# Layer 0, attention heads 8 to 15: VectorE's low halves of the turned probabilities before the biased maxima two heads on

## The chip, the cores and the metric

The kernel runs on one core of one Trainium2 chip. The metric is device time in microseconds (us) of one execution. The kernel before took 1215.46 us, the median of three runs (1212.08 to 1216.16).

## The reference, cut to what matters

A two-layer decoder trunk on 512 tokens of width 1024, in float32. Layer 0 mixes eight heads of full causal attention with a forget gate (kind A, heads 0 to 7) and eight heads of attention over a sliding window of 128 tokens with a sink and a bias by distance (kind B, heads 8 to 15). The change lies in the stretch of kind B:

```python
logits = jnp.einsum("bnqhgd,bnkhd->bnhgqk", qb, kb) * (d ** -0.5)
logits = jnp.where(mask, logits + bias, -jnp.inf)
sink = jnp.broadcast_to(sinks..., logits.shape[:-1] + (1,))
p = jax.nn.softmax(jnp.concatenate([logits, sink], axis=-1), axis=-1)[..., :-1]
out = jnp.einsum("bnhgqk,bnkhd->bnqhgd", p, vb)
```

The outputs of all sixteen heads go through one output projection, then a squared-ReLU MLP; layer 1 is another mixer and another MLP, and a norm ends it.

## The kernel before, in words

Nothing of the order is planned by a program: each engine has its instructions written out by hand in one in-order stream, and semaphores (`wait_ge`, `then_inc`) tie the streams together. Float32 precision comes from halves: a value is split into a rounded high half (ScalarE, a copy to fp32r, line 1191) and the low half that is left (a subtraction, on VectorE at line 1806 or on GpSimd at line 1628), and TensorE multiplies the halves one after the other. GpSimd also makes the low halves of the weights (wl, 128x1024 each).

Layer 0's attention is run in steps s = -2 to 15; every engine has its own `first_step(s)`. For s from 8 to 15 the step holds, on each engine in this order:

- TensorE (L1012): the scores of head s+2 (L830, L831; they wait for the exponentials of head s+1), the projection slabs of the step (only the last one, slab 18, in step 8) or some tiles of the output projection (`OUT_TILES_AT`, L711 to L713: nine matmuls in each of the steps 9 to 14, six in step 15), the values of head s (L901 with the high halves of the turned probabilities, L902 with the low halves; each bank waits for `pt_lo`), and the transposes of the probabilities of head s+1 (L891; they wait for `probs_ready`).
- ScalarE (L1421): half of the output of head s-1 from its bank (sq, `o_half`), the high halves of head s (probT_h, `pt_hi`), the high half of an earlier output, the exponentials of head s+2 (L1372, four instructions in two banks, and a small one for the sink at L1370, `exp_done`), and in steps 8, 10 and 12 the high half of one weight slab (128x1024).
- VectorE (L2054): the two halves of the output of head s-1 summed (L2045, `o_sum`), `maxima(s + 2)` (L1991: four custom instructions at L2006 that add the bias strip to the scores in their bank and take the row extremum, `max_ready`), `probs_lo(s)` (L2031: two subtractions at L1806, `pt_lo`), `normalise(s + 2)` (L2024: `sums` at L2021 and L2022, which wait for the exponentials of head s+2, then four multiplications at L2029, `probs_ready`), and in steps 7 to 9 the low half of a projected query and its slab (L1806, L1863).
- GpSimd: in steps 8, 10 and 12 the low half of a weight slab, then in even steps the low half of an output pair (128x512, ur<-sq,ur).
- SyncE: weight loads and the bias strips (L641); the strip of head j waits for the maxima of head j-2.

The maxima of head s+2 exist in this place for s = 8 to 13 only (the condition `NH <= s and s + 2 < 2 * NH`, with NH = 8). In steps below 8 the maxima stand in a later place of the step, and steps 14 and 15 have none. Behind step 15 come the last tiles of the output projection, whose later weights are loaded once the last transposes are done (L682, L683, L609).

Of the kernel before, what the change touches and what calls it, by code (L numbers as in the profile page):

```python
# [43 lines left out]
NH = 8  # L44
# [102 lines left out]
def trunk(nc, x, norm_mix_e, w_in_e, b_forget, sink_logits, w_out_e, norm_mix_o, w_in_o, norm_cq, norm_ckv,  # L147
          w_uq, w_ukv, w_out_o, norm_mlp, w_mlp1, w_mlp2, rel_bias, norm_final,
          c_onehot, c_fixed, c_rope, out):
    with ExitStack() as ctx:  # L150
# [279 lines left out]
        def units(j):  # L430
            if attention(j) == "B":
                return [(0, 0, 0, 128, 0), (1, 0, 128, 256, 128), (2, 1, 0, 256, 384), (3, 1, 256, 256, 640)]
            return [(0, 0, 0, 128, 0), (2, 0, 128, 384, 128), (1, 1, 0, 256, 512), (3, 2, 0, 512, 768)]
# [4 lines left out]
        def attention(j):  # L438
            return "ABDC"[j // NH]
# [4 lines left out]
        def banks_before(j):  # L444

            return sum(score_banks(i) for i in range(j))
# [48 lines left out]
        def placed(n):  # L495

            return n + 1 if n < FA else n
# [11 lines left out]
        def slabs_of(s):  # L509
            return SLABS_AT.get(s, ())  # L510
# [18 lines left out]
        def strip_count(j):  # L529

            return sum(1 for i in range(j + 1) if attention(i) in "BC" and i % 2 == j % 2)
# [1266 lines left out]
        def _(dve):  # L1798
# [51 lines left out]
            def take_slab(n, scale=1.0, dst=None):  # L1850
                dve.wait_ge(slab_done, n + 1)
                if n in (N_IN1 + 2, N_IN1 + 3, N_IN1 + 4) and dst is None:
                    dve.wait_ge(p_hi, SPLIT0 + n - N_IN1 - 1)
                    if n == N_IN1 + 2:
                        dve.wait_ge(ki_lo, 1)
                        dve.wait_ge(ki_spread, 1)
                    else:
                        dve.wait_ge(qi_lo, n - N_IN1 - 2)
                elif n >= N_IN1 + 2 and dst is None:
                    dve.wait_ge(p_lo, SPLIT0 + n - N_IN1 - 4)  # L1860
                elif 2 <= n < N_OUT0 and n - 2 != FA and dst is None:
                    dve.wait_ge(p_lo, placed(n - 2))
                v.scalar_tensor_tensor(tbuf[:, n % 2, :] if dst is None else dst, pj(n)[:, :], scale, rstd[:, :], ALU.mult, ALU.mult)\  # L1863
                    .then_inc(slab_taken, 1)
# [126 lines left out]
            def maxima(j):  # L1991
                if j >= 2:
                    dve.wait_ge(exp_done, banks_before(j - 1))
                us, slot = units(j), j % 2
                biased = attention(j) in "BC"
                if biased:
                    dve.wait_ge(strip_loaded[slot], 16 * strip_count(j))
                if j == NH:
                    dve.wait_ge(sink_ready, 1)
                for i, (blk, b, col, w, _) in enumerate(us):  # L2000
                    dve.wait_ge(scores_ready, banks_before(j) + b + 1)
                    logits, neg = bank[b][:, col:col + w], negmax[:, slot, blk:blk + 1]
                    if biased:
                        width = 2 * W if attention(j) == "B" else S
                        limit = sink_neg[:, j % NH:j % NH + 1] if attention(j) == "B" else -TAKEN
                        m = v.tensor_tensor_reduce(logits, logits, strip_raw[:, slot, width - w:width], -1.0, limit,  # L2006
                                                   ALU.add, ALU.min, neg)
                    else:
                        m = v.reduce_max(neg, logits, AX.X, negate=True)  # L2009
                    if i + 1 == len(us) or us[i + 1][1] != b:  # L2010
                        m.then_inc(max_ready, 1)

            def sums(j):

                dve.wait_ge(exp_done, banks_before(j + 1))
                if j >= 2 * NH + 2:
                    dve.wait_ge(diag_made, j - 2 * NH - 1)
                elif j >= 2:
                    dve.wait_ge(probs_ready, 4 * (j - 1))
                if attention(j) == "B":  # L2020
                    own.link(v.tensor_tensor(sink_exp[:, j % 2, :], sink_exp[:, j % 2, :], expsum[:, j % 2, :], ALU.add))  # L2021
                v.reciprocal(rsum[:, j % 2, :], (sink_exp if attention(j) == "B" else expsum)[:, j % 2, :]).then_inc(rsum_ready, 1)  # L2022

            def normalise(j):  # L2024
                sums(j)
                dve.wait_ge(rsum_ready, j + 1)
                for blk, _, _, w, pc in units(j):
                    pr = probs[:, j % 2, pc:pc + w]
                    v.tensor_scalar(pr, pr, rsum[:, j % 2, blk:blk + 1], None, ALU.mult).then_inc(probs_ready, 1)  # L2029

            def probs_lo(s, parts=range(3)):  # L2031

                for k, (b, c0, w) in enumerate(pt_banks(s)):
                    if k not in parts:
                        continue
                    dve.wait_ge(pt_hi, pt_before(s) + k + 1)
                    c = slice(512 * k, 512 * k + w)
                    sub(probT_l[:, c], bank[b][:, c0:c0 + w], probT_h[:, c]).then_inc(pt_lo, 1)

            def outputs_summed(s):  # L2040

                _, r = out_tile(s)
                dve.wait_ge(o_half, s + 1)
                o = o_f32(s)[r:r + HD, :]
                v.tensor_tensor(o, out_bank(s)[HD:P, :], o, ALU.add).then_inc(o_sum, 1)  # L2045
# [8 lines left out]
            def first_step(s):  # L2054

                if 1 <= s:
                    outputs_summed(s - 1)
                if NH <= s and s + 2 < 2 * NH:
                    maxima(s + 2)
                if 0 <= s:  # L2060
                    probs_lo(s, range(2))
                if NH <= s and s + 2 < 2 * NH:
                    normalise(s + 2)
                if s < NH:
                    if 0 <= s:
                        probs_lo(s, (2,))
                    maxima(s + 2)
                    if 0 <= s + 1:
                        normalise(s + 1)
                for n in slabs_of(s - 1):  # L2070
                    if n not in V_INSIDE:
                        projected(placed(n) - 1, EVEN[n][0], n)
                for n in slabs_of(s):
                    take_slab(n, HD ** -0.5 if EVEN[n][0][0] == "q" else 1.0)
                    if n in V_INSIDE:
                        projected(placed(n) - 1, EVEN[n][0], n)
                if s == NH - 1:
                    normalise(NH + 1)
# [91 lines left out]
            for s in FIRST_STEPS:  # L2170
                first_step(s)
# [105 lines left out]
```

## Time and profile before

| what | before |
|---|---|
| median of three runs | 1215.46 us (1212.08 to 1216.16) |
| the profiled execution | 1216.44 us, span 1214.6 us |
| TensorE (matmul) busy | 1166.6 us, 96% |
| VectorE busy | 678.1 us, 56% |
| ScalarE busy | 505.5 us, 42% |
| GpSimd busy | 523.1 us, 43% |
| steps 8 to 15 of the attention | about 161 to 213 us after the span's start |

The span runs from the first to the last instruction of the profiled execution, whose own time is 1.8 us more. In rows of instructions the first column is the start in us from the span's start, the second the time the group lasted; "xN" is the number of instructions merged in a row, and the bracket at the end is the idle time of the engine ahead of it and who ended it. In output<-input the names are the program's. The custom maxima show as CUSTOM_DVE_ANT_0.

### The profile page before, as it was taken

What the parts mean: (1) busy time and instruction counts of PE and PEld (TensorE: products, weight loads), DVE (VectorE), ACT (ScalarE), POOL (GpSimd) and SP (SyncE); (2) the same over time, 40 slices, a digit from 0 to 9 for tenths busy, and PEclk for the clock granted to TensorE, in tenths of its full rate; (3) what the DMA queues carried; (4) which work ended last, traced back from release to release, by engine and by line L of the source; (5) the groups of instructions that cost most, each with busy time, mean ns of one, the idle gap of its engine ahead of it and who ended that gap; (6) DMA issues with size and microseconds to landing.
All of it is one profiled execution on the core that took longest, in us unless ns stands there. A gap on an engine that the chain in (4) does not pass through costs nothing.

```text
span 1214.6 us, 15797 instructions
## 1 busy us (share of the span) xinstructions
PE 1166.6 (96%) x5601; PEld 959.5 (79%) x5605; DVE 678.1 (56%) x1094; ACT 505.5 (42%) x910; POOL 523.1 (43%) x267
## 2 busy tenths in 40 slices
PE   7999988999999999999997899989999999999997
PEld 5788877878888888888765778878788888888886
DVE  5866697664154163265569798737651541631654
ACT  6677665432222132134373377844321321322233
POOL 2433322444444444447643375224444444444441
PEclk9999998999999999999998999999999999999999
DMA  5233331333333333333322100103333333333332
GB/s 158 72 108 94 98 114 46 110 88 100 103 88 105 89 101 99 91 104 87 88 69 70 35 19 27 45 18 87 87 104 90 102 100 91 104 88 102 92 98 87
DMA packets 191225, 104.94 MB, mean 86 GB/s; under 512 B 9062, under 2 KB 187537, under 8 KB 191170
## 3 DMA queue, kind: packets, MB, share of 16 engines
q1 hardware_dynamic: 189900, 104.09, 29.8%
q8 instruction: 33, 0.54, 0.2%
q10 hardware_dynamic: 1270, 0.13, 0.1%
q14 instruction: 22, 0.18, 0.0%
HBM read 102.04 MB, written 6.35 MB: 89 GB/s over the span
## 4 chain that ended last, share of the span: by engine, by line
PE 81%; DVE 9%; ACT 5%; issue 3%; POOL 1%; DMA 1%; SPq 0%; DVEq 0%; ACTq 0%
PE bank L711 25%; PE bank L713 25%; PE bank L712 25%; ACT probs L1372 2%; PE bank L889 2%; DVE probT_l L1806 1%; POOL wl L1628 1%; PE bank L891 1%; PE bank L901 1%; ACT ur L1191 1%; PE bank L902 1%; DVE score L2127 1%; ACT wh L1191 1%; DVE best L2123 1%; DVE probs L2029 1%
## 5 line engine op out<-in xcount | busy, mean ns | idle before, releaser
L1628 POOL TENSOR_TENSOR wl<-raw,wh 128x1024 fp32r<-128x1024 f32 x171 | 417.8, 2444 | 550.0 <-ACT wh L1191 550.0
L711 PE MATMUL bank<-ur,wh 128*128 128x512 f32 x1072 | 418.5, 390 | 0.3 <-POOL wl L1628 0.3
L713 PE MATMUL bank<-ur,wl 128*128 128x512 f32 x1072 | 417.1, 389 | 0.0
L712 PE MATMUL bank<-ur,wh 128*128 128x512 f32 x1072 | 417.1, 389 | 0.0
L1191 ACT ACTIVATE wh<-raw 128x1024 fp32r<-128x1024 f32 x171 | 180.8, 1058 | 509.4 <-PE bank L713 509.2
L711 PEld LDWEIGHTS bank<-ur,wh 128*128 128x128 f32 x1072 | 201.4, 188 | 43.1 <-issue 1.6
L712 PEld LDWEIGHTS bank<-ur,wh 128*128 128x128 f32 x1072 | 201.3, 188 | 42.1 <-issue 0.5
L713 PEld LDWEIGHTS bank<-ur,wl 128*128 128x128 f32 x1072 | 201.2, 188 | 41.6
L1970 DVE TENSOR_TENSOR xT<-bank,xT 128x512 f32<-128x512 f32 x64 | 44.3, 692 | 227.7 <-PE bank L713 227.5
L1806 DVE TENSOR_TENSOR ur<-sq,ur 128x512 fp32r<-128x512 f32 x65 | 129.8, 1997 | 45.4 <-ACT ur L1191 45.4
L711 PE MATMUL bank<-xh,wh 128*128 128x512 f32 (+1 forms) x296 | 123.5, 417 | 7.8 <-POOL xl L1628 3.0
L712 PE MATMUL bank<-xl,wh 128*128 128x512 f32 (+1 forms) x296 | 117.9, 398 | 0.0
L713 PE MATMUL bank<-xh,wl 128*128 128x512 f32 (+1 forms) x296 | 117.5, 397 | 0.0
L1961 DVE TENSOR_TENSOR tbuf<-bank,rstd 128x512 f32<-128x512 f32 x64 | 44.2, 691 | 92.1 <-PE bank L713 91.6
L711 PEld LDWEIGHTS bank<-xh,wh 128*128 128x128 f32 (+1 forms) x296 | 56.6, 191 | 24.6 <-issue 8.5
L1372 ACT ACTIVATE probs<-bank,negmax 128x256 f32<-128x256 f32 (+3 forms) x128 | 63.4, 506 | 27.4 <-DVE negmax L2009 15.2
L1191 ACT ACTIVATE ur<-sq 128x512 fp32r<-128x512 f32 (+1 forms) x80 | 50.6, 633 | 45.9 <-DVE sq L1965 38.5
L713 PEld LDWEIGHTS bank<-xh,wl 128*128 128x128 f32 (+1 forms) x296 | 56.7, 192 | 13.3
L712 PEld LDWEIGHTS bank<-xl,wh 128*128 128x128 f32 (+1 forms) x296 | 57.0, 192 | 12.7 <-issue 1.5
L1870 DVE TENSOR_TENSOR sqsum<-sqsum,sq 128x512 f32<-128x512 f32 x28 | 46.0, 1642 | 18.8 <-ACT sq L1230 18.8
L1806 DVE TENSOR_TENSOR probT_l<-bank,probT_h 128x512 fp32r<-128x512 f32 (+1 forms) x88 | 48.8, 599 | 12.6 <-ACT probT_h L1191 12.4
L1191 ACT ACTIVATE ur<-tbuf 64x512 fp32r<-64x512 f32 (+2 forms) x68 | 42.3, 628 | 26.4 <-DVE tbuf L2108 14.6
(223 smaller groups left out, 1291.6 us busy)
## 6 DMA issues: line engine op xcount, KB each, us to landing
raw<-in_w_mlp SPq DMA_DIRECT2D x128, 512.0 KB, 3.9
raw<-in_w_in_e SPq DMA_DIRECT2D x18, 512.0 KB, 3.7
raw<-in_w_in_o SPq DMA_DIRECT2D x10, 512.0 KB, 3.7
raw<-in_w_out_e SPq DMA_DIRECT2D x8, 512.0 KB, 4.0
raw<-in_w_out_o SPq DMA_DIRECT2D x8, 512.0 KB, 3.7
skew_c<-bias_rows SPq DMA_DIRECT2D x8, 319.5 KB, 4.6
strip_raw<-skew_c SPq DMA_DIRECT2D x8, 256.0 KB, 2.6
skew_b<-bias_rows SPq DMA_DIRECT2D x8, 191.5 KB, 4.0
```

Of the source, the lines that this page charges most:

```text
L711: mm(dst, lhs[0], rhs[0], start=start, stop=False, skip_group_check=not check)
L712: mm(dst, lhs[0], rhs[1], start=False, stop=False, skip_group_check=not check)
L713: return mm(dst, lhs[1], rhs[0], start=False, stop=stop, skip_group_check=not check)
L889: done = mm(dst, probs[:, slot, c:c + P], diag[slot][:, q:q + P], start=True, stop=True)
L891: done = nc.tensor.transpose(dst, probs[:, slot, c:c + P], ident[:, :])
L1191: return nc.scalar.activation(dst, src, ACT.Copy, scale=scale)
L1372: e = nc.scalar.activation(probs[:, slot, pc:pc + w], bank[b][:, col:col + w], ACT.Exp, bias=negmax[:, slot, blk:blk + 1], scale=sign, acc ...
L1628: return nc.gpsimd.tensor_tensor(dst, a, b, ALU.subtract)
L1806: return v.tensor_tensor(dst, a, f(b), ALU.subtract)
L1870: v.tensor_tensor(sqsum[:, :], sqsum[:, :], sq[:, m % 2, :], ALU.add).then_inc(sq_added, 1)
L1961: v.tensor_tensor(t, ps, rstd[:, :], ALU.mult).then_inc(slab_taken, 1)
L1970: v.tensor_tensor(xT[:, m, :], ps, xT[:, m, :], ALU.add).then_inc(slab_taken, 1)
```

## The change

In `first_step` of VectorE the call of `maxima(s + 2)` is moved from ahead of `probs_lo(s, range(2))` to behind it, directly ahead of `normalise(s + 2)`. The condition is the same. No instruction, wait or transfer is added or dropped, and no other engine's stream changes.

```diff
@@ -2055,11 +2055,10 @@
 
                 if 1 <= s:
                     outputs_summed(s - 1)
-                if NH <= s and s + 2 < 2 * NH:
-                    maxima(s + 2)
                 if 0 <= s:
                     probs_lo(s, range(2))
                 if NH <= s and s + 2 < 2 * NH:
+                    maxima(s + 2)
                     normalise(s + 2)
```

## Rows read from the trace of the kernel before

**Rows 1.** The page, busy time of each engine over the span.
```profile
PE 1166.6 (96%) x5601; PEld 959.5 (79%) x5605; DVE 678.1 (56%) x1094; ACT 505.5 (42%) x910; POOL 523.1 (43%) x267
```
**Rows 2.** Waits, 145 to 215 us: us in total, times, longest.
```profile
PE bank L901 <- DVE probT_l L1806: 8.8, 4, 3.8
...
DVE sink_exp L2021 <- ACT probs L1372: 2.1, 6, 0.5
```
**Rows 3.** The chain that ended last, step 11: start, us, what.
```profile
184.94 0.69 DVE sq L2045
...
187.30 0.56 DVE probT_l L1806
187.99 0.37 PE bank L901
```
**Rows 4.** Timeline of VectorE, step 9.
```profile
170.70 0.69 DVE L2045 TENSOR_TENSOR sq<-bank,sq 64x512 f32<-64x512 f32 x1
171.43 0.36 DVE L2006 CUSTOM_DVE_ANT_0 bank<-bank,strip_raw,sink_neg 128x128 f32<-128x128 f32 x1
...
172.92 1.15 DVE L1806 TENSOR_TENSOR probT_l<-bank,probT_h 128x512 fp32r<-128x512 f32 x2
174.55 0.16 DVE L2021 TENSOR_TENSOR sink_exp<-sink_exp,expsum 128x4 f32<-128x4 f32 x1 [0.48 <-ACT probs L1372]
...
174.97 1.07 DVE L2029 TENSOR_SCALAR probs<-probs,rsum 128x128 f32<-128x128 f32 x4
176.07 1.39 DVE L1806 TENSOR_TENSOR ur<-tbuf,ur 64x512 fp32r<-64x512 f32 x2
```
**Rows 5.** Timeline of VectorE, its idle times in steps 12 and 14.
```profile
190.40 0.69 DVE L2045 TENSOR_TENSOR sq<-bank,sq 64x512 f32<-64x512 f32 x1 [0.29 <-ACT sq L1191]
192.12 0.36 DVE L2006 CUSTOM_DVE_ANT_0 bank<-bank,strip_raw,sink_neg 128x128 f32<-128x128 f32 x1 [1.02 <-PE bank L831]
...
204.49 0.69 DVE L2045 TENSOR_TENSOR sq<-bank,sq 64x512 f32<-64x512 f32 x1 [0.47 <-ACT sq L1191]
205.37 1.15 DVE L1806 TENSOR_TENSOR probT_l<-bank,probT_h 128x512 fp32r<-128x512 f32 x2 [0.19 <-ACT probT_h L1191]
```
**Rows 6.** Timeline of TensorE, first value matmul of steps 9, 11, 13 and 14.
```profile
173.75 0.36 PE L901 MATMUL bank<-probT_h,ur 128*128 128x256 f32 x1 [3.85 <-DVE probT_l L1806]
...
187.99 0.37 PE L901 MATMUL bank<-probT_h,ur 128*128 128x256 f32 x1 [2.15 <-DVE probT_l L1806]
...
201.89 0.55 PE L901 MATMUL bank<-probT_h,ur 128*128 128x256 f32 x1 [2.43 <-DVE probT_l L1806]
...
207.28 0.28 PE L901 MATMUL bank<-probT_h,ur 128*128 128x256 f32 x1
```
**Rows 7.** Busy time by stretch; the number behind POOL is the granted clock.
```profile
178.00:179.00 1.00, 1.00 (x7) 0.83 (x6) 0.95 (x4) 0.63 (x1) 0.00 (x0) 1.00 0.01 5
189.00:191.00 2.00, 2.00 (x12) 2.00 (x11) 1.68 (x6) 0.93 (x2) 0.00 (x0) 0.50 0.86 249
```
**Rows 8.** Timeline of ScalarE, high halves of weights, steps 8 and 10.
```profile
165.32 1.06 ACT L1191 ACTIVATE wh<-raw 128x1024 fp32r<-128x1024 f32 x1 [0.41 <-PE bank L713]
...
181.13 1.07 ACT L1191 ACTIVATE ur<-raw 128x1024 fp32r<-128x1024 f32 x1
```
**Rows 9.** Timeline of GpSimd, steps 8 and 10.
```profile
166.46 2.94 POOL L1628 TENSOR_TENSOR wl<-raw,wh 128x1024 fp32r<-128x1024 f32 x1 [6.03 <-ACT wh L1191]
169.36 1.71 POOL L1628 TENSOR_TENSOR ur<-sq,ur 128x512 fp32r<-128x512 f32 x1
182.28 2.48 POOL L1628 TENSOR_TENSOR ur<-raw,ur 128x1024 fp32r<-128x1024 f32 x1 [11.21 <-ACT ur L1191]
```
**Rows 10.** Timeline of VectorE beside those GpSimd instructions.
```profile
166.46 3.49 DVE L1806 TENSOR_TENSOR ur<-tbuf,ur 64x512 fp32r<-64x512 f32 x2
...
181.69 3.22 DVE L2029 TENSOR_SCALAR probs<-probs,rsum 128x128 f32<-128x128 f32 x4
```
**Rows 11.** Timeline of SyncE's queue behind the last transposes.
```profile
209.15 0.38 SPq L682 DMA_DIRECT2D probs<-in_w_uq  x1
...
210.14 12.27 SPq L609 DMA_DIRECT2D raw<-in_w_out_e  x3
```
**Rows 12.** Timeline of TensorE, output projection, the first marked idle behind step 15.
```profile
231.40 0.47 PE L711 MATMUL bank<-ur,wh 128*128 128x512 f32 x1 [0.26 <-POOL wl L1628]
```

## The prediction

> **What bounds the kernel now.** First the page: TensorE is busy for 96% of the span [rows 1], so time can be gained only in the few places where it stands still, and lost wherever it is made to stand still. Then the waits of the stretch from 145 to 215 us, which holds the changed steps: there TensorE's value matmuls wait four times, 8.8 us in all, for VectorE's low halves [rows 2]. That is what the moved call seems to serve. But the wait names only the last releaser. The chain shows what lies behind it: in step 11 it runs along VectorE from the output sum at 184.94 through the maxima to the low half at 187.30, and only then to TensorE at 187.99 [rows 3]. So I read VectorE's own stream over a whole step, to see whether the low halves are late because of the maxima alone, or because VectorE is late as a whole.
>
> Step 9 is the plain one [rows 4]. The output sum starts at 170.70, the maxima 0.73 us later at 171.43, the low halves at 172.92 for 1.15 us; then VectorE idles 0.48 us for ScalarE's exponentials, makes the sums at 174.55, and normalises from 174.97 for 1.07 us. From the start of the maxima to the start of the sums is 174.55 - 171.43 = 3.12 us. This is a chain through two engines: maxima, exponentials, sums. The low halves lie inside it, in time in which VectorE would otherwise wait. All that is spare in the step is 0.48 us. Over the six steps 8 to 13 the waits before the sums come to 2.1 us [rows 2], so in the five others it is (2.1 - 0.48) / 5 = 0.32 us. In this stretch VectorE with that chain is the bound, and TensorE waits for it.
>
> **The change, part by part.** Nothing is added or removed; six calls of the maxima (steps 8 to 13) go behind two low halves each. No DMA is moved on its queue. SyncE's strip for the head two further on waits for these maxima and comes later with them, but has more than 6 us before it is used (the output sums of steps 12 and 14, two steps apart, lie 14.1 us apart [rows 5]).
>
> What is won: in each of the six steps the low halves start earlier by the length of the maxima, 172.92 - 171.43 = 1.49 us [rows 4] to 1.6 us, as the high halves of the head are ready by then in most steps.
>
> What is lost: the maxima start later by the two low halves, 1.15 us and 0.04 us of turnaround, 1.19 us in all. Their exponentials start and end later by the same amount, and so do the sums and the normalising, since nothing on VectorE is left to fill the wait: its idle time there goes from some 0.35 us to some 1.5 us. As the next step's sum of outputs stands behind the normalising in the same stream, the whole next step is later too. So the loss adds up from step to step, and the gain does not. Six steps: 6 x 1.19 = 7.1 us at the end of step 13.
>
> What takes up part of it [rows 5]: in step 12 VectorE idles 0.29 us for ScalarE's half of the output and 1.02 us for the scores; work that is late by more than that finds no wait there, so 1.31 us come back. In step 14 it idles 0.47 us and 0.19 us: 0.66 us. Then TensorE: in step 14 it starts its value matmuls at 207.28 without a wait [rows 6], whereas the low half began at 205.37. In step 9 TensorE started 173.75 - 172.92 = 0.83 us behind the start of the low half, so here it could have started at 206.20, and has 1.08 us of room. Together 3.05 us. Loss at the value matmuls of step 14: 7.14 - 3.05 = 4.1 us. In steps 14 and 15 no maxima are left and nothing changes.
>
> Check against the steps between: the values of step 9 come a little earlier or about level (late by what step 8 loses, 1.2 us, early by 1.5 us [rows 4]); those of step 11 are late by 3 x 1.19 - 1.6 = 2.0 us, those of step 13 by 5 x 1.19 - 1.31 - 1.6 = 3.0 us. TensorE's waits of 3.85, 2.15 and 2.43 us [rows 6] therefore stay in sum.
>
> **GpSimd in step 8** is the part that I can only bound. VectorE instructions between on-chip tiles are held up while GpSimd works: the four normalising instructions of step 10 take 3.22 us beside a weight's low half of 2.48 us [rows 9, 10], as against 1.07 us in step 9 [rows 4], and two projected low halves take 3.49 us as against 1.39 us [rows 4, 10]. In steps 10 and 12 both sides are released by the same exponentials, so the collision moves as it stands: no cost. In step 8 ScalarE's weight half starts at 165.32, released by TensorE [rows 8]; with the exponentials 1.19 us later it starts right behind them, as it does in step 10 at 181.13. Then the last normalising instruction of step 8 meets GpSimd as in step 10 (2.15 us more), the projected low halves meet it no longer (2.10 us less), unless GpSimd's next instruction, the output's low half of 1.71 us [rows 9], meets them in turn. Between nothing and 1.4 us; both engines are engaged the whole time, and I take the middle, 0.7 us.
>
> The Trainium skill ("SBUF — State Buffer", the section on the shared port pair) says that a VectorE instruction in a two-port mode, or with two inputs in SBUF, and a GpSimd instruction exclude each other for a whole instruction, whichever starts first. By that rule both collisions in step 8 would happen in full, and the sum would be 4.1 + 1.4 = 5.5 us; that is the upper end of the bound above.
>
> **Downstream.** The shift passes on in full. Behind step 15 TensorE has no marked idle until 0.26 us at 231.40 [rows 12], and the loads of the later output weights are issued behind the last transposes, from 209.15 [rows 11], so they move along.
>
> **Sum:** 4.1 + 0.7 = 4.8 us over the profiled execution, 1216.44 to 1221.2 us. That execution lies 1.0 us over the median of the runs shown, so against 1215.46 us I forecast 1220.3 us, slower by 0.4%. About 0.3%, 3.6 us here, is what a measurement of this kernel can tell from no change: the forecast lies only just outside.
>
> **Rivals.** *TensorE's side decides (faster).* If VectorE had room, TensorE's waits would shrink by the 1.6 us that the low halves come earlier, in steps 9, 11 and 13, and by the fourth wait of the list, 8.8 - 3.85 - 2.15 - 2.43 = 0.4 us in step 10: 3 x 1.6 + 0.4 = 5.2 us, giving 1210.3 us. A second gain goes with it: behind waits of over 2 us TensorE runs at a granted clock of 0.50, that is 1.2 GHz (189 to 191 us), and at 1.00, 2.4 GHz, elsewhere [rows 7]; shorter waits could spare that. For it speaks the wait list [rows 2]. Against it speaks that VectorE idles only 0.32 to 0.48 us in the place where 1.19 us would be needed. It decides from the point at which the idle ahead of the sums exceeds 1.19 us. Chance 0.08, with a further 0.02 for smaller gains.
>
> *Absorbed.* More of the loss is taken up than I count: ScalarE could work off its copies of outputs and high halves before the delayed exponentials, and a step whose values start earlier has its scores earlier, as in step 12, where the maxima wait for them. If half of the 7.1 us is recovered rather than 3.05 us and step 8 costs nothing, 3.5 us remain; if two steps are free, 1.7 us. 1217 to 1219 us. That also holds if the order as it runs does not differ in effect, for instance if the low halves wait for high halves in some steps. Chance 0.30.
>
> *TensorE's clock as the price (much slower).* The longer idles let the clock fall in steps 14 and 15 too, where it did not before. The transposes, tiles and values from 207.28 to 211 would then run at half speed for 2 to 4 us (the stretch of 2 us from 189 us is such a one) and cost half of that, some 1.5 us more: 6.3 us, 1221.8 us; with both collisions of step 8, as the rule on the port pair has them, some 7 us, 1222.5 us. Chance 0.15 for the two together. The forecast itself gets 0.45.
>
> **How the numbers follow.** The absorbed case is mostly under 3.6 us, the forecast's lower part (4.1 us, less the scatter of a median of about 1 us) partly so. So: faster 0.10, within 0.3% 0.31, slower 0.59. The range goes from 1214.5 us, where most of the absorbed case is in, to 1223.5 us, the two late prices together and the scatter of the runs; the faster case is left out.
>
> **What the changed profile would show.** If I am right: VectorE's idle ahead of the sums (line 2021) grows from 0.32 to about 1.5 us in all six steps, 2.1 us in total to some 9; the low halves stand directly behind the output sum; the distance from one step's output sum to the next grows by about 1.2 us in steps 8 to 11 and 13; TensorE's wait for the low halves stays at 8 us or more; the idle at line 2006 of step 12 is gone; the last transposes' release of SyncE moves from 209.15 to about 214 us. Wrong would be the forecast if that idle stays under 1 us, if TensorE's wait for the low halves falls to 5 us or less, or if the later stretch gives the shift back by a wait that shrinks.

## The result, and the profile after

The changed kernel takes 1220.56 us, the median of seven runs (1218.50 to 1222.39), beside 1215.46 us for the kernel before. The ratio is 1.0052, with a 95% interval from 1.0039 to 1.0064. A second series (e10 below) gave 1219.83 us and a ratio of 1.0040 (1.0026 to 1.0053). The change makes the kernel slower by about 0.4 to 0.5%.

The page has the same busy times as before [rows 1], to within 2.0 us on every engine; only the span is longer, 1218.6 us. So the time went into idle time. The page's first line of engines after:

```profile
PE 1166.3 (96%) x5605; PEld 957.5 (79%) x5605; DVE 679.3 (56%) x1094; ACT 505.0 (41%) x910; POOL 521.9 (43%) x267
```

The waits from 145 to 220 us (us in total, times, longest) answer to rows 2. TensorE's wait for the low halves is 8.8 us as it was, now in six pieces; VectorE's wait ahead of the sums has gone from 2.1 to 8.0 us. And TensorE has a new wait, for GpSimd's low half of a spare weight slab:

```profile
PE bank L901 <- DVE probT_l L1806: 8.8, 6, 4.3
...
DVE sink_exp L2021 <- ACT probs L1372: 8.0, 6, 1.3
...
PE bank L711 <- POOL ur L1628: 1.4, 1, 1.4
```

VectorE in step 9, as in rows 4. The low halves now start 0.72 us behind the output sum, the maxima behind them, and the idle ahead of the sums is 1.32 us where it was 0.48 us:

```profile
174.05 0.69 DVE L2045 TENSOR_TENSOR sq<-bank,sq 64x512 f32<-64x512 f32 x1
174.77 1.16 DVE L1806 TENSOR_TENSOR probT_l<-bank,probT_h 128x512 fp32r<-128x512 f32 x2
175.84 0.35 DVE L2006 CUSTOM_DVE_ANT_0 bank<-bank,strip_raw,sink_neg 128x128 f32<-128x128 f32 x1
...
178.79 0.16 DVE L2021 TENSOR_TENSOR sink_exp<-sink_exp,expsum 128x4 f32<-128x4 f32 x1 [1.32 <-ACT probs L1372]
...
179.20 1.07 DVE L2029 TENSOR_SCALAR probs<-probs,rsum 128x128 f32<-128x128 f32 x4
```

The distances between the output sums (line 2045) on VectorE show where the time went. They are worked out from the starts of those rows, in us:

| from step to step | 8-9 | 9-10 | 10-11 | 11-12 | 12-13 | 13-14 | 14-15 | 15-end | sum |
|---|---|---|---|---|---|---|---|---|---|
| before | 9.56 | 6.79 | 7.45 | 5.46 | 8.45 | 5.64 | 4.56 | 3.34 | 51.25 |
| changed | 11.52 | 7.67 | 8.38 | 6.27 | 8.39 | 6.27 | 3.41 | 3.35 | 55.26 |
| difference | +1.96 | +0.88 | +0.93 | +0.81 | -0.06 | +0.63 | -1.15 | +0.01 | +4.01 |

I call the sum the stretch: from the output sum in step 8 (161.14 us before, 162.53 us after) to the last one (212.39 and 217.79 us). It is 4.0 us longer. It repeats well: the second profile of each kernel (e11, e10) has 51.20 and 55.19 us. The rest of the span behind it (span less the start of the last output sum) ranges from 1000.6 to 1004.6 us over all profiles of this study, though no experiment touches it; the last section shows where. So the experiments are read by the stretch first and by the time second. Each experiment's stretch comes from one profile.

Step 8 holds the largest piece. GpSimd's rows first, then VectorE's beside them; they answer to rows 9 and 10:

```profile
168.27 2.49 POOL L1628 TENSOR_TENSOR wl<-raw,wh 128x1024 fp32r<-128x1024 f32 x1 [6.45 <-ACT wh L1191]
170.73 1.31 POOL L1628 TENSOR_TENSOR ur<-sq,ur 128x512 fp32r<-128x512 f32 x1
```

```profile
167.69 3.23 DVE L2029 TENSOR_SCALAR probs<-probs,rsum 128x128 f32<-128x128 f32 x4
170.95 2.35 DVE L1806 TENSOR_TENSOR ur<-tbuf,ur 64x512 fp32r<-64x512 f32 x2
```

The normalising meets the weight's low half (3.23 us, before 1.07 us), and the projected low halves meet GpSimd's second instruction (2.35 us, where 1.39 us is their time alone). Together 5.58 us, against 1.07 + 3.49 = 4.56 us before: 1.02 us of collision, the rest of the 1.96 us is the order.

On TensorE's side (rows 6) the waits of steps 9, 13 and 14 are these:

```profile
175.61 0.55 PE L901 MATMUL bank<-probT_h,ur 128*128 128x256 f32 x1 [4.31 <-DVE probT_l L1806]
...
206.32 0.35 PE L901 MATMUL bank<-probT_h,ur 128*128 128x256 f32 x1 [2.37 <-DVE probT_l L1806]
...
212.59 0.36 PE L901 MATMUL bank<-probT_h,ur 128*128 128x256 f32 x1 [0.71 <-DVE probT_l L1806]
```

The loads behind the last transposes (rows 11) start at 214.54, 5.4 us later. Of that, 1.39 us were lost in this execution ahead of step 8, where both kernels are the same:

```profile
214.54 0.38 SPq L682 DMA_DIRECT2D probs<-in_w_uq  x1
```

### The profile page after: what moved, and what is told of

It is laid out like the page before. It is cut to its first block, busy times and chain, and to the rows that moved or that the text cites. A ratio compares the mean times of both kernels' runs of the same rounds, so it can differ in the third digit from the quotient of the medians.

```text
span 1218.6 us, 15801 instructions
## 1 busy us (share of the span) xinstructions
PE 1166.3 (96%) x5605; PEld 957.5 (79%) x5605; DVE 679.3 (56%) x1094; ACT 505.0 (41%) x910; POOL 521.9 (43%) x267
## 4 chain that ended last, share of the span: by engine, by line
PE 78%; DVE 12%; ACT 5%; issue 3%; POOL 1%; DMA 1%; SPq 0%; DVEq 0%; ACTq 0%
PE bank L711 25%; PE bank L713 24%; PE bank L712 24%; ACT probs L1372 2%; DVE probT_l L1806 2%; DVE score L2126 1%; DVE probs L2029 1%; PE bank L889 1%; POOL wl L1628 1%; DVE best L2122 1%; PE bank L891 1%; ACT ur L1191 1%; DMA score<-in_x 1%; ACT wh L1191 1%; PE bank L901 1%
## 5 line engine op out<-in xcount | busy, mean ns | idle before, releaser
L713 PEld LDWEIGHTS bank<-xh,wl 128*128 128x128 f32 (+1 forms) x296 | 56.5, 191 | 13.1
```

Source lines behind the costliest of these rows:

```text
L713: return mm(dst, lhs[1], rhs[0], start=False, stop=stop, skip_group_check=not check)
```

## The experiments

| run | what | stretch, us | against 51.25 | median, us | ratio to before (95%) |
|---|---|---|---|---|---|
| e1 | new order in steps 8 to 10 | 54.67 | +3.4 | 1218.87 | 1.0050 (1.0033 to 1.0068) |
| e2 | new order in steps 11 to 13 | 51.46 | +0.2 | 1215.74 | 1.0032 (1.0016 to 1.0047) |
| e3 | new order in step 11 | 49.51 | -1.7 | 1213.54 | 1.0003 (0.9987 to 1.0018) |
| e4 | old order, spare weights early | 44.36 | -6.9 | 1209.67 | 0.9965 (0.9952 to 0.9978) |
| e5 | changed, work in VectorE's wait | 56.47 | +5.2 | 1219.72 | 1.0041 (1.0029 to 1.0054) |
| e6 | before, work ahead of the maxima | 57.61 | +6.4 | 1223.94 | 1.0072 (1.0047 to 1.0096) |
| e7 | changed, spare weights early | 54.29 | +3.0 | 1220.65 | 1.0050 (1.0032 to 1.0069) |
| e8 | e4, head 9 normalised earlier | 45.57 | see below | 1209.67 | 0.9947 (0.9924 to 0.9970) |
| e9 | e8, first spare slab in step 10 | 45.13 | see below | 1208.17 | 0.9948 (0.9930 to 0.9965) |
| e10 | changed, again | 55.19 | +3.9 | 1219.83 | 1.0040 (1.0026 to 1.0053) |
| e11 | before, again | 51.20 | 0.0 | 1214.68 | 1.0003 (0.9992 to 1.0014) |

The median of before was 1214.32 us beside e1 to e4 and 1214.57 us beside the others.

**The theory** is that of the prediction: VectorE and its chain through ScalarE's exponentials is the bound; the low halves used to lie inside that chain's wait. The rivals are that each step of the new order simply costs its share, that GpSimd's collisions or TensorE's clock make the loss, and that TensorE's late low halves count.

**e1 and e2: the order in three steps each.**

```diff
-                if NH <= s and s + 2 < 2 * NH:
+                if NH <= s and s + 2 < 2 * NH and s not in (8, 9, 10):
                     maxima(s + 2)
                 if 0 <= s:
                     probs_lo(s, range(2))
+                if s in (8, 9, 10):
+                    maxima(s + 2)
                 if NH <= s and s + 2 < 2 * NH:
                     normalise(s + 2)
```

e2 has (11, 12, 13) in place of (8, 9, 10).

> The maxima go behind the low halves in steps 8, 9 and 10 only. Measured from the start of the output sum of step 8 to that of the last one (51.25 us before, 55.26 us with the change in all six steps). Theory (VectorE and its chain through the exponentials is the bound, each step loses 1.19 us there, a loss is given back only where something waits): three steps lose 3.6 us, step 8's collisions with GpSimd add up to 1.3 us, and in steps 11 and 12, in the old order, nothing is given back: 3.5 to 4.8 us longer, nearly the whole loss. Rival (each step of the new order costs the same share of 4.0 us): 2.0 us. Rival (TensorE's late low halves count): shorter than before.

> The new order in steps 11, 12 and 13 only. Theory: 3.6 us of loss at the end of step 13, but the early low half of step 11 spares TensorE its wait and so VectorE's wait for the scores in step 12 (1.0 us) and for the output (0.3 us), and at the end 0.7 us of VectorE's idle and 1.1 us of TensorE's room take up more: 0 to 1 us longer. Rival (same share for each step): 2.0 us longer.

Measured: +3.4 us and +0.2 us. Equal shares would have been 2.0 us each, so that rival falls. In e1 the idle ahead of the sums is 1.33 us in a step of the new order (8) and 0.32 us in one of the old (11):

```profile
165.61 0.16 DVE L2021 TENSOR_TENSOR sink_exp<-sink_exp,expsum 128x4 f32<-128x4 f32 x1 [1.33 <-ACT probs L1372]
...
192.10 0.16 DVE L2021 TENSOR_TENSOR sink_exp<-sink_exp,expsum 128x4 f32<-128x4 f32 x1 [0.32 <-ACT probs L1372]
```

Steps 8 to 10 have no wait that could take up the loss. Steps 11 to 13 have, in steps 12 and 14. The times of whole runs agree in order, but both ratios are higher than the stretch alone would make them: 0.2 us is 0.02%, and e2's interval begins at 0.16%. By the medians that difference is 1.1 to 1.2 us in e1, e2 and the change, by the ratios 2.3 to 3.7 us. Its cause is open.

**e3: the order in step 11 alone.** The diff is that of e1 with (11,).

> The new order in step 11 only. Theory: the low half of step 11 comes 1.6 us earlier, VectorE's stream 1.19 us later; in step 12 the maxima wait 1.0 us for scores that TensorE makes late, at 1.2 GHz, behind a wait of 2.15 us; that wait shrinks to 0.5 us, so step 12 takes up the loss: 1.5 us shorter to no change. Rival (each step costs): 0.7 to 1.2 us longer.

Measured: the stretch is 1.7 us shorter than before, for two reasons. The first is the one expected. In step 12 VectorE finds the output's half and the scores ready; the output sum has no wait, nor have the maxima (0.29 us and 1.02 us before [rows 5]), and step 12 takes 7.45 instead of 8.45 us. As step 11 takes 0.8 us more, this wins 0.2 us:

```profile
190.55 0.69 DVE L2045 TENSOR_TENSOR sq<-bank,sq 64x512 f32<-64x512 f32 x1
```

The other 1.55 us are won in steps 13 and 14 (5.20 and 3.45 us, before 5.64 and 4.56 us), where the order is the old one in both kernels. TensorE waits 2.43 us for the low half of step 13 in both. In the kernel before the granted clock is 0.52 on average from 201.89 to 205.40, behind this wait; the level of 0.50 is 1.2 GHz, and at 1.00, 2.4 GHz, TensorE runs again from about 205.4:

```profile
204.00:206.00 2.00, 2.00 (x11) 1.87 (x10) 1.34 (x4) 1.65 (x4) 0.00 (x0) 0.69 0.00 0
```

So the values of step 14 start 5.39 us behind those of step 13 (201.89 and 207.28 [rows 6]). In e3 the clock stays at 1.00 and it is 3.82 us:

```profile
201.05 0.36 PE L901 MATMUL bank<-probT_h,ur 128*128 128x256 f32 x1 [2.43 <-DVE probT_l L1806]
...
204.87 0.28 PE L901 MATMUL bank<-probT_h,ur 128*128 128x256 f32 x1
```

Both profiles of the kernel before have this fall of the clock, and e1 has it too. Whether the order of step 11 or chance spared it in e3 is open. The time of whole runs does not show a gain (ratio 0.9987 to 1.0018), so as a faster kernel e3 is not proven; 1.7 us is 0.14%.

**e4: the old order, with the spare weight slabs' halves a step earlier.** This takes GpSimd's long instruction away from the normalising of steps 10 and 12.

```diff
-SPARE_AT = {10: 21, 12: 22}
+SPARE_AT = {9: 21, 11: 22}
...
                 if 0 <= s:
                     probs_hi(s, range(2))
+                if s in SPARE_AT:
+                    split_spare(SPARE_AT[s], (o_ready, NH))
                 placed_before(s, (0,))
...
-                if s in SPARE_AT:
-                    split_spare(SPARE_AT[s], (o_ready, NH))
```

> The old order; the halves of the two spare weight slabs are made a step earlier (ScalarE behind its high halves in steps 9 and 11, GpSimd with them), where VectorE works from its banks in PSUM. Theory: the four normalising instructions of steps 10 and 12 take 1.07 us, not 3.22 us; as VectorE is the bound there, the stretch gets shorter by 4.3 us or more (up to 7 us, since TensorE's waits of over 2 us and the slow clock behind them shrink too). Rival (GpSimd's collision is hidden behind TensorE's tiles or ScalarE): under 1 us.

Measured: 6.9 us off the stretch, and the kernel faster, 1209.67 us against 1214.32 us. The normalising of steps 10 and 12 takes 1.07 us:

```profile
181.29 1.07 DVE L2029 TENSOR_SCALAR probs<-probs,rsum 128x128 f32<-128x128 f32 x4
...
192.02 1.07 DVE L2029 TENSOR_SCALAR probs<-probs,rsum 128x128 f32<-128x128 f32 x4
```

Two times 2.15 us of held-up VectorE is 4.3 us. Of the other 2.6 us, 1.0 us is the wait for the scores of step 12. Some 1.55 us come in steps 13 and 14, as in e3: TensorE waits only 0.30 us for the low half of step 13 where it waited 2.43 us, and its clock does not fall behind that. The list of waits from 155 to 222 us has 5.5 us where it was 8.8 us, and no wait of step 12 for scores:

```profile
PE bank L901 <- DVE probT_l L1806: 5.5, 5, 3.8
```

This confirms from the other side that VectorE was the bound. The whole time fell by less than the stretch, 0.9965 with at best 0.9952, that is 5.8 us. Where the rest lies is open; the scatter outside the stretch, in the last section, is of that size.

**e5: work in the wait of the changed order.** The two added lines are:

```diff
                 if NH <= s and s + 2 < 2 * NH:
                     maxima(s + 2)
+                    v.tensor_tensor(score[:, 0:512], rstd[:, :], rstd[:, :], ALU.mult)
+                    v.tensor_tensor(score[:, 512:768], rstd[:, 0:256], rstd[:, 0:256], ALU.mult)
                     normalise(s + 2)
```

> The changed kernel, with two multiplications whose result nothing uses (128x512 and 128x256, on VectorE, some 1.1 us together) between the maxima and the sums in steps 8 to 13. Theory: VectorE idles 1.33 us there for ScalarE's exponentials, so 6.6 us of work cost nothing: the stretch stays at 55.3 us within 0.3 us. Rival (VectorE's work as such is the bound, or the exponentials start late for another reason): up to 6.6 us longer.

Step 9 of e5 on VectorE:

```profile
175.38 0.69 DVE L2062 TENSOR_TENSOR score<-rstd 128x512 f32<-128x512 f32 x1
175.98 0.41 DVE L2063 TENSOR_TENSOR score<-rstd 128x256 f32<-128x256 f32 x1
176.84 0.16 DVE L2021 TENSOR_TENSOR sink_exp<-sink_exp,expsum 128x4 f32<-128x4 f32 x1 [0.45 <-ACT probs L1372]
```

The added work fits into the idle time, 0.45 us of which is left. From the output sum of step 8 to that of step 14 it is 48.49 us, against 48.50 us in the changed kernel: six times 0.9 us of VectorE's time for nothing. That is a little less than the low halves (1.07 us from their start to the maxima), which the change took out of this place. The expectation missed in one point: the stretch is 56.5, not 55.3 us, by 1.2 us that arise behind step 14. They are TensorE's clock, below.

**e6: the same work ahead of the maxima in the kernel before.** The maxima are late and the low halves too.

```diff
                 if NH <= s and s + 2 < 2 * NH:
+                    v.tensor_tensor(score[:, 0:512], rstd[:, :], rstd[:, :], ALU.mult)
+                    v.tensor_tensor(score[:, 512:768], rstd[:, 0:256], rstd[:, 0:256], ALU.mult)
                     maxima(s + 2)
```

> The kernel before, with the same two multiplications ahead of the maxima in steps 8 to 13: the maxima are as late as in the changed order, but the low halves are late too. Theory: what the change loses on VectorE without what it wins on TensorE's side: 6 to 7 us longer than the 51.25 us of before, so 2 to 3 us worse than the change. Rival (the change costs something of its own, GpSimd's collision or the clock, not the maxima's delay): well under 4 us longer.

Measured: 6.4 us longer, 2.4 us more than the change. TensorE's wait for the low halves, from 155 to 225 us:

```profile
PE bank L901 <- DVE probT_l L1806: 14.0, 4, 6.5
```

So delaying the maxima is enough to make the loss. Of the 2.4 us by which e6 is worse than the change, 0.7 us arise up to the output sum of step 14 (49.23 us against 48.50 us). The other 1.6 us lie between steps 14 and 15, where TensorE's clock fell to 0.50 in e6 and its values of step 14 start without a wait at 213.25, 5.41 us behind those of step 13. So the earlier low halves of the change give back 0.7 us for certain; that the 1.6 us belong to them as well is not shown.

**e7: the changed order with the spare weights early.** The move of e4, in the changed kernel.

> The changed order with the spare weight slabs' halves a step earlier, to be compared with the same move in the old order (44.36 us, e4). Theory: with the collisions of steps 10 and 12 gone the bound is VectorE's chain all the more, with less idle time to take up losses; 51 to 54 us, that is 7 to 9 us longer than e4, more than the 4.0 us that the change costs in the kernel before. Rival (the loss is that of the order alone and stays): 48.4 us.

Measured: 54.29 us, 9.9 us more than e4; a little beyond what was expected. Both slabs' collisions with the normalising are gone, but in step 8 GpSimd's added instruction meets the projected low halves that are late there already. The distance from the output sum of step 8 to that of step 9 is 13.55 us, where the changed kernel has 11.52 us. The rows of TensorE in step 9:

```profile
175.83 0.55 PE L901 MATMUL bank<-probT_h,ur 128*128 128x256 f32 x1 [6.35 <-DVE probT_l L1806]
```

This step costs 4.0 us against e4. Each of the steps 9 to 13 takes 0.8 to 1.1 us more than in e4, 4.7 us together: with the waits gone that could take it up, the loss by the order comes back in every step. The last 1.2 us lie behind step 14, where TensorE's clock had fallen:

```profile
210.00:212.00 2.00, 2.00 (x9) 1.90 (x9) 1.20 (x2) 1.68 (x3) 0.00 (x0) 0.50 0.00 0
```

So most of what e4's move wins in the old order is lost again in the changed one.

**e8 and e9: the way on from e4.** Head 9 is normalised in step 7 before the projected halves, ahead of GpSimd's weight slab 19; e9 has SPARE_AT = {10: 21, 11: 22} besides.

```diff
                     if 0 <= s + 1:
                         normalise(s + 1)
+                    if s == NH - 1:
+                        normalise(NH + 1)
...
-                if s == NH - 1:
-                    normalise(NH + 1)
```

> e4, and in step 7 the normalising of head 9 is moved from the end of VectorE's step to right behind that of head 8, ahead of GpSimd's low half of weight slab 19, which holds it up by 2.2 us at its old place. Measured from the start of the stretch's first common point, the transposes of step 7, and by the whole time. Theory: VectorE reaches step 8 2.4 us earlier, the projected low halves of step 8 no longer meet GpSimd (2.1 us), and TensorE's wait of 3.84 us in step 9 shrinks below 1 us: 3 to 4 us shorter than e4 in all, some 10 us shorter than before. Rival (TensorE's slab 18, which ends where it did, sets step 9): no change against e4.

> e8 with the first spare slab's halves made in step 10 instead of step 9, in both cases behind ScalarE's high halves. In e8 that 1.05 us stood ahead of the exponentials of step 9, and VectorE idled 1.96 us before the sums there. Theory (VectorE's chain through the exponentials is the bound, whoever delays it): the wait before the sums in step 9 falls to about 1.0 us or less, GpSimd's weight half of step 10 lies beside VectorE's work from its banks, and TensorE's wait of 3.26 us in step 10 shrinks: 1 to 2 us shorter than e8 in the stretch. Rival: ScalarE's order in step 9 did not matter; no change against e8 (0.3 us).

The stretch starts with step 8, so these two are measured from the output sum of step 7: before 63.09, e4 56.20, e8 54.98, e9 54.58 us. e8 wins 1.2 us instead of 3 to 4 us. The output sum of step 9 does come 3.6 us sooner (17.78 us behind that of step 7, in e4 21.39 us), but 2.4 us are given back. ScalarE had the spare slab's copy ahead of the exponentials of step 9; e8:

```profile
173.33 0.16 DVE L2021 TENSOR_TENSOR sink_exp<-sink_exp,expsum 128x4 f32<-128x4 f32 x1 [1.96 <-ACT probs L1372]
```

and e9, with that copy a step later:

```profile
172.10 0.16 DVE L2021 TENSOR_TENSOR sink_exp<-sink_exp,expsum 128x4 f32<-128x4 f32 x1 [1.34 <-ACT probs L1372]
```

The wait shrinks by 0.6 us and the stretch by 0.4 us, nearer to the rival's 0.3 us than to the 1 to 2 us expected: in e9 TensorE still waits 2.83 us in step 10, where it waited 3.26 us in e8. Both are faster than either kernel of the case; 1208.17 us for e9 is the lowest median, though its interval overlaps those of e4 and e8.

**e10 and e11: both kernels again.**

> The changed kernel once more. From the output sum of step 8 to the last one it took 55.26 us in its profile; in e5, with the same times on VectorE up to step 14, it took 56.47 us, since TensorE's granted clock was 0.50 in the values and transposes of step 14 there, and 0.50 some 3 us earlier, in tiles ahead of a wait, in the first. Theory: where the clock falls differs from execution to execution; up to step 14 this profile shows the same 48.5 us, and the whole 55.3 or 56.5 us. Rival: it is the added work of e5 that made the difference, so 55.3 us again.

> The kernel before once more: from the output sum of step 8 to the last one 51.25 us, within 0.3 us, and the same on VectorE in every step; the times of whole runs scatter by more than that (1210.75 to 1217.72 us so far), so the scatter has to come from outside these steps. Rival: the stretch itself scatters by a microsecond, then the differences between single profiles mean no more than that.

The stretches came out as 55.19 and 51.20 us. The last output sums, behind the first ones at 160.66 and 161.01, are e10:

```profile
215.85 0.69 DVE L2045 TENSOR_TENSOR sq<-bank,sq 64x512 f32<-64x512 f32 x1 [1.46 <-ACT sq L1191]
```

and e11:

```profile
212.21 0.69 DVE L2045 TENSOR_TENSOR sq<-bank,sq 64x512 f32<-64x512 f32 x1 [1.47 <-ACT sq L1191]
```

TensorE's clock differs all the same. These are stretches of the changed kernel, of e5 and of e10; the number behind POOL is the granted clock. The changed kernel, tiles ahead of the values of step 14:

```profile
208.00:209.00 1.00, 1.00 (x5) 0.90 (x4) 0.18 (x2) 1.00 (x6) 0.00 (x0) 0.50 0.00 0
```

e5, values and transposes of step 14 and the tiles behind them:

```profile
212.00:214.00 2.00, 2.00 (x12) 2.00 (x11) 0.69 (x1) 1.10 (x2) 0.00 (x0) 0.50 0.00 0
```

e10, the same place:

```profile
212.00:214.00 2.00, 1.98 (x12) 1.36 (x10) 1.46 (x3) 1.97 (x4) 0.00 (x0) 1.00 0.23 38
```

In the changed kernel the clock is at 1.2 GHz in tiles that end in a wait, which costs nothing; in e10 it did not fall there at all, at waits of the same length; in e5 it fell where nothing waits and cost 1.2 us. e5 and e10 reach the values of step 14 alike, 50.05 and 50.01 us behind the output sum of step 8. Whether e5's added work moves the chance of that fall is open; the clock as such is enough for the difference.

## Why the prediction was right, point by point

The forecast, 1220.3 us, slower, was met by 1220.56 us. Its steps fared unequally, and the close match is partly luck: the profiles' stretch grew by 4.0 us, not by 4.8 us. In the forecast's own terms the six steps lost 5.9 us (7.1 forecast), 2.9 us were taken up (3.05) and the collisions of step 8 cost 1.0 us (0.7). A loss sized 1.2 us too high stood in for 1.1 us of the medians that the changed steps do not explain.

**The bound was read rightly.** The low halves lay in VectorE's wait for the exponentials. The idle ahead of the sums grew from 2.1 to 8.0 us where "some 9" was forecast; e5 shows that the place is free, e6 that the delay of the maxima makes the loss, e4 that time taken off VectorE in these steps comes off the whole, and e7 against e4 that the loss repeats in each step.

**The loss per step was sized too high.** The term was 1.19 us; the idle grew by 1.0 us (from 0.32 to 1.33 us) where no other wait interferes, and the steps 9 and 10 became longer by 0.88 and 0.93 us. Step 9's own idle had been 0.48, not 0.32 us, since ScalarE was still at a copy of an output (172.00 to 172.63) when the first maximum was ready. And the maxima start while the low halves end: they start 1.07 us behind the low halves' start (174.77 and 175.84), not 1.19 us.

**What takes it up was placed rightly.** Step 12 costs nothing (-0.06 us), step 13 costs 0.63 us since the 0.47 us of idle behind it is used up, and between steps 14 and 15 1.15 us come back, where 1.08 us of TensorE's room and 0.19 us of VectorE's idle had been counted. e1 and e2, 3.4 and 0.2 us, show the same by halves. e3 shows more than was forecast: the early low half can also remove a wait of VectorE's next step.

What the forecast did not ask is why TensorE had 1.08 us of room in step 14. It is the slow clock of step 13 in the kernel before, which held up the values of step 14 by some 1.57 us (5.39 against 3.82 us, see e3). Had the clock stayed up there, the kernel before would have been some 1.55 us shorter, and the change would have cost some 5.5 us of the stretch; this is an estimate from e3. How often the clock falls there in the runs that have no profile is open.

**GpSimd in step 8** was bounded by 0 and 1.4 us and taken at 0.7 us; the rows give 1.02 us. Both collisions took place. By the Trainium skill ("SBUF — State Buffer", "Who interferes with whom") the first of the two instructions holds the shared ports for its whole length and the other is blocked. The trace nearly agrees: VectorE's projected halves, issued at 170.95, end at 173.30; from GpSimd's end at 172.04 that is 1.26 us, 0.13 us less than the 1.39 us that they take alone. The prediction does not work out its upper bound of 1.4 us. With 1.71 us for GpSimd's second instruction, as before, in place of the 1.31 us measured, the rows would give 1.42 us.

**Sum.** 5.15 us of loss up to step 14 and 1.15 us given back make 4.0 us. Against the median 5.1 us were measured, and in the second series 4.9 us by the ratio, with intervals that reach from 3.2 to 7.8 us. 4.0 us lies within the second interval and below the first. The rest is not explained by the changed steps.

**The rivals.** TensorE as the bound (faster) falls with the 8.8 us that stayed; a local form of it is true in step 11 (e3). "Absorbed" was right in kind, in steps 12 and 14 only. The clock as a price was not paid in the two profiles of the changed kernel, but was in e5 and e7 (1.2 us each), in the steps that the prediction named.

**Missed altogether:** GpSimd's spare slab of step 10 comes 3.8 us later against the output sum of step 8, and TensorE waits 1.4 us for it in a tile of step 11. It costs nothing only because the low half of that step is later still. The prediction said of that collision that it moves as it stands, and did not name who waits for the slab.

## What to carry to other kernels

A wait list names the last releaser, not the bound. Before an instruction is brought forward on an in-order engine, look at what lies behind it in that stream: if it is the head of a chain through another engine (maxima, exponentials, sums), the work that stood in the chain's wait was free and is free no longer, and the loss repeats with each step while the gain does not. Count waits that could take up the loss with care: some of them may be there only because TensorE's clock had fallen.

Where the engine that is the bound is held up by another's instruction, moving that other one by a step can be worth more than its own order: here 6.9 us of the stretch against 4.0 us lost by the order. Measure a stretch between two instructions of the same line; it repeated within 0.1 us where the rest of the span scattered by 4 us.

## What the runs showed of the hardware

Two executions of the kernel before differ by 1.8 us in their span (1214.6 and 1212.8 us). Of this, 1.6 us lie in one place in layer 1, behind a stretch in which TensorE is busy for 1.5 of 4 us. In the next 4 us, within VectorE's wait for the last output sum (9.6 and 8.0 us), the granted clock was 0.57 in one and 1.00 in the other. The kernel before:

```profile
802.00:806.00 4.00, 1.50 (x7) 1.24 (x8) 1.46 (x3) 1.08 (x2) 1.26 (x1) 1.00 0.00 0
806.00:810.00 4.00, 4.00 (x12) 3.17 (x11) 0.00 (x0) 0.00 (x0) 0.00 (x0) 0.57 0.00 0
```

and e11, the same kernel:

```profile
801.70:805.70 4.00, 1.50 (x6) 1.23 (x7) 1.46 (x3) 1.08 (x2) 1.26 (x1) 1.00 0.00 0
805.70:809.70 4.00, 4.00 (x19) 3.30 (x18) 0.00 (x0) 0.00 (x0) 0.00 (x0) 1.00 0.00 0
```

The same idle time ahead, and the clock falls in one execution and not in the other. The changed kernel had it both ways as well: 37.9 us in its first profile and 39.5 us in e10 between two output sums of layer 1 that frame this place, with 39.5 us and 37.9 us in the two of the kernel before.

A second such place stands at the start of layer 1, behind a stretch of 4 us in which TensorE is busy for 2.4 us. From VectorE's memset of `score` to its copy of the norm (`rstd`) it takes 6.7 us in six of the thirteen profiles, among them both first ones and e11; 8.3 us in five, among them e10; and 9.9 us in two, e6 and e7. In e11, e10 and e6 the granted clock of the 3.5 us that begin 1.5 us behind the memset was 1.00, 0.64 and 0.50. Between the stretch and this place all thirteen profiles agree to 0.1 us (386.4 us). So the scatter of the rest, 1000.6 to 1004.6 us, comes mainly from these two places; each is worth 1.6 us, the second also twice that.

VectorE's instructions on tiles in SBUF are held up as a whole: the fourth normalising instruction of step 10 in the kernel before started 0.14 us behind GpSimd's (182.42 and 182.28) and took 2.49 us, where the first two together took 0.55 us. The instructions that read a bank in PSUM beside GpSimd kept their time, as the output sum of step 9 before, 0.69 us at 170.70 beside GpSimd's instruction from 169.36 to 171.07.
